# Every phase of a transformer trunk puts the moving operands of its matmuls at another place within 256 bytes

## The reference, cut to what matters

```
for i in range(DEPTH):                                   # 4
    x = x + 0.5 * _swiglu(_rms_norm(x, norm_ffn1[i]), w_gate, w_up, w_down)
    y = mixer(_rms_norm(x, norm_mix[i]))                 # fox, conv, diff, fox
    x = x + y
    x = x + 0.5 * _swiglu(_rms_norm(x, norm_ffn2[i]), w_gate, w_up, w_down)

def _swiglu(h, w_gate, w_up, w_down):                    # D = 1024, D_FF = 2816
    return (jax.nn.silu(h @ w_gate) * (h @ w_up)) @ w_down
```

## Time and profile before

| | us |
|---|---|
| median of 2 runs (1982.21 and 1983.81) | 1983.01 |
| the profiled execution | 1984.66 |
| its span, first to last instruction | 1982.9 |
| TensorE busy in the span | 1955.8 |
| VectorE busy | 1423.5 |
| ScalarE busy | 1044.5 |
| mean granted TensorE clock, share of full speed | 0.996 |

### The profile page before, as it was taken

One profiled execution on the slowest core, in us unless ns is written; L12 is line 12 of the kernel. 1 busy time (PEld: TensorE's weight loads), 2 busy tenths in 40 slices (PEclk: granted clock), 3 DMA queues, 4 the chain that ended last, 5 costly groups with the idle time before them and its releaser, 6 DMA issues.

```text
span 1982.9 us, 29095 instructions
## 1 busy us (share of the span) xinstructions
PE 1955.8 (99%) x12575; PEld 1714.5 (86%) x12575; DVE 1423.5 (72%) x1647; ACT 1044.5 (53%) x1251; POOL 100.8 (5%) x114
## 2 busy tenths in 40 slices
PE   8999999999999998999999999999999999999999
PEld 7888889888888895988888888788888888889887
DVE  8875778875877555876587658887758765778763
ACT  6544656554554444654465455575436544566542
POOL 3000001000200001100100000010000000001000
PEclk9999999999999998999999999999999999999999
DMA  7656435655665683565666553356565655435653
GB/s 243 193 181 193 138 130 166 191 186 189 196 192 181 195 245 74 191 191 187 195 191 191 182 180 128 108 180 191 182 195 187 192 184 179 147 128 172 191 189 108
DMA packets 336669, 350.14 MB, mean 177 GB/s; under 512 B 10125, under 2 KB 331934, under 8 KB 336542
## 3 DMA queue, kind: packets, MB, share of 16 engines
q1 hardware_dynamic: 332046, 343.58, 54.2%
q10 hardware_dynamic: 4496, 4.70, 1.2%
HBM read 346.04 MB, written 2.22 MB: 176 GB/s over the span
## 4 chain that ended last, share of the span: by engine, by line
PE 92%; DVE 3%; ACT 2%; DMA 1%; issue 1%; POOL 1%; ACTq 0%; SPq 0%; DVEq 0%; POOLq 0%
PE banks L1477 49%; PE banks L1482 24%; PE banks L1468 5%; PE banks L1470 4%; PE banks L1469 4%; PE banks L1699 1%; PE banks L1752 1%; DMA u_away<-sb_u_pad 1%; PE banks L1940 1%; DVE sb_w_low L825 1%; PE banks L1719 1%; PE banks L1736 1%; ACT sb_w_high L479 0%; DMA sb_raw<-in_ffn_w_gate 0%; ACT sb_scores L617 0%
## 5 line engine op out<-in xcount | busy, mean ns | idle before, releaser
L825 DVE TENSOR_TENSOR sb_w_low<-sb_raw,sb_w_high 128x2048 fp32r<-128x2048 f32 (+1 forms) x331 | 750.7, 2271 | 209.0 <-ACT sb_w_high L479 208.4
L1477 PE MATMUL banks<-sb_x_both,sb_w_high 128*128 128x512 f32 x2816 | 721.3, 393 | 0.9 <-issue 0.9
L479 ACT ACTIVATE sb_w_high<-sb_raw 128x2048 fp32r<-128x2048 f32 (+1 forms) x331 | 616.5, 1867 | 128.2 <-DMA sb_raw<-in_ffn_w_down 111.2
L1477 PEld LDWEIGHTS banks<-sb_x_both,sb_w_high 128*128 128x128 f32 x2816 | 499.0, 188 | 81.7 <-issue 1.2
L1482 PEld LDWEIGHTS banks<-sb_x_both,sb_w_low 128*128 128x128 f32 x2792 | 385.9, 188 | 35.4
L1482 PE MATMUL banks<-sb_x_both,sb_w_low 128*128 128x256 f32 x2792 | 394.0, 278 | 0.0
L1477 PE MATMUL banks<-sb_h_both,sb_w_high 128*128 128x512 f32 x1408 | 360.1, 394 | 0.0
L1477 PEld LDWEIGHTS banks<-sb_h_both,sb_w_high 128*128 128x128 f32 x1408 | 250.2, 188 | 45.7
L1482 PEld LDWEIGHTS banks<-sb_h_both,sb_w_low 128*128 128x128 f32 x1408 | 190.7, 188 | 17.1
L1482 PE MATMUL banks<-sb_h_both,sb_w_low 128*128 128x256 f32 x1408 | 194.2, 278 | 0.0
L1468 PE MATMUL banks<-sb_x_both,sb_w_high 128*128 128x256 f32 x512 | 146.9, 287 | 0.0
(11 more groups left out here) (235 smaller groups left out, 1943.5 us busy)
## 6 DMA issues: line engine op xcount, KB each, us to landing
sb_raw<-in_ffn_w_up SPq DMA_DIRECT2D x88, 1024.0 KB, 5.4
sb_raw<-in_ffn_w_gate SPq DMA_DIRECT2D x87, 1024.0 KB, 5.4
sb_raw<-in_ffn_w_down SPq DMA_DIRECT2D x64, 1024.0 KB, 5.0
sb_raw<-in_ffn_w_down SPq DMA_DIRECT2D x32, 768.0 KB, 4.3
sb_raw<-in_fox_w_in SPq DMA_DIRECT2D x24, 1024.0 KB, 5.3
sb_raw<-in_conv_w_pw SPq DMA_DIRECT2D x12, 1024.0 KB, 5.5
sb_raw<-in_diff_w_in SPq DMA_DIRECT2D x12, 1024.0 KB, 5.1
sb_raw<-in_fox_w_out SPq DMA_DIRECT2D x8, 1024.0 KB, 4.9
```

Source lines behind the costliest of these rows:

```text
L479: act.activation(slot(w_high, b)[:, 0:width(b)], slot(raw, b)[:, 0:width(b)], ACT.Copy).then_inc(S["high_ready"], 1)
L825: dve.tensor_tensor(slot(w_low, b)[:, 0:width(b)], slot(raw, b)[:, 0:width(b)], slot(w_high, b)[:, 0:width(b)].bitcast(F32), ALU.subtract) ...
L1477: return pe.matmul(pair(bank[at][:, :]), high[:, n * P:(n + 1) * P], m_both, start=first, stop=last, skip_group_check=True)
```

## The change

`x_both` becomes one of 12 views, one for each phase, into `x_room`, a tensor that is 256 elements longer than `x_both` with its shift, and `h_both` one of 12 views into `h_room`. A place is a number of 4-byte elements from the room's beginning. Nothing else is changed: the same instructions in the same order, the same waits, the same transfers.

```
-        sb("shift_x", [P, 16])
-        x_both = sb("x_both", [P, 2, KT, SEQ], F32R)
-        x_high, x_low = x_both[:, 0, :, :], x_both[:, 1, :, :]
+        x_room = sb("x_room", [P, 4368], F32R)
...
-        sb("shift_h", [P, 200])
         with ExitStack() as during_ffn:
-            h_both = during_ffn.enter_context(nc.sbuf_tensor("sb_h_both", [P, 2, FF_TILES, SEQ], F32R))
+            h_room = during_ffn.enter_context(nc.sbuf_tensor("sb_h_room", [P, 11592], F32R))
...
-        sb("shift_o", [P, 24])
...
+        def both_parts_at(room, tiles, place):
+            first, adjacent, apart = place
+            size = tiles * SEQ
+            if adjacent:
+                return room[:, first:first + 2 * size].rearrange("p (t a n) -> p a t n", a=2, n=SEQ)
+            parts = room[:, first:first + 2 * (size + apart)].rearrange("p (a r) -> p a r", a=2)
+            return parts[:, :, 0:size].rearrange("p a (t n) -> p a t n", n=SEQ)
+
+        X_HOME, H_HOME = (16, False, 0), (200, False, 0)
+        X_PLACE = {0: (4, False, 0), 2: (8, False, 0), 3: (12, False, 0), 5: (20, False, 0), 6: (24, False, 0),
+                   8: (28, False, 0), 9: (40, False, 0), 11: (56, False, 0),
+                   4: (48, False, 0), 7: (8, False, 0), 10: (48, False, 0)}
+        H_PLACE = {0: (40, False, 0), 2: (32, False, 0), 3: (36, False, 0), 5: (44, False, 0), 6: (48, False, 0),
+                   8: (28, False, 0), 9: (0, False, 0), 11: (16, False, 0)}
+        x_both = [both_parts_at(x_room, KT, X_PLACE.get(i, X_HOME)) for i in range(len(phases))]
+        h_both = [both_parts_at(h_room, FF_TILES, H_PLACE.get(i, H_HOME)) for i in range(len(phases))]
...
-                    act.activation(x_high[:, t, :], src, ACT.Copy, scale=vec[:, col + t:col + t + 1]
+                    act.activation(x_both[i][:, 0, t, :], src, ACT.Copy, scale=vec[:, col + t:col + t + 1]
...
-                    return both_parts(pair_banks(p) + 2 * which + n, n, high, low, lambda k: x_both[:, :, k, :],
+                    return both_parts(pair_banks(p) + 2 * which + n, n, high, low, lambda k: x_both[i][:, :, k, :],
...
-                        ins = both_parts(2 * (T % 2) + n, n, high, low, lambda k: h_both[:, :, first + k, :],
+                        ins = both_parts(2 * (T % 2) + n, n, high, low, lambda k: h_both[i][:, :, first + k, :],
```

More of the change, by code:

```diff
@@ L570, in high @@
                     act.wait_ge(S["hidden_ready"], PAIRS * f + p + 1)
-                    act.activation(h_both[:, 0, 2 * p:2 * p + 2, :], pair(hidden[:, :]), ACT.Copy
+                    act.activation(h_both[i][:, 0, 2 * p:2 * p + 2, :], pair(hidden[:, :]), ACT.Copy
                                    ).then_inc(S["h_high_ready"], 1)
@@ L869, in x_lows @@
                     src = xT[:, t, :] if i else bank[T][:, t % 2 * SEQ:t % 2 * SEQ + SEQ]
-                    dve.scalar_tensor_tensor(x_low[:, t, :], src, vec[:, col + t:col + t + 1],
-                                             x_high[:, t, :].bitcast(F32), ALU.mult, ALU.subtract
+                    dve.scalar_tensor_tensor(x_both[i][:, 1, t, :], src, vec[:, col + t:col + t + 1],
+                                             x_both[i][:, 0, t, :].bitcast(F32), ALU.mult, ALU.subtract
                                              ).then_inc(S["xlow_ready"], 1)
@@ L1035, in low @@
                     dve.wait_ge(S["h_high_ready"], PAIRS * f + p + 1)
-                    dve.tensor_tensor(h_both[:, 1, 2 * p:2 * p + 2, :], pair(hidden[:, :]),
-                                      h_both[:, 0, 2 * p:2 * p + 2, :].bitcast(F32),
+                    dve.tensor_tensor(h_both[i][:, 1, 2 * p:2 * p + 2, :], pair(hidden[:, :]),
+                                      h_both[i][:, 0, 2 * p:2 * p + 2, :].bitcast(F32),
                                       ALU.subtract).then_inc(S["h_low_ready"], 1)
@@ L1494, in both_parts, with x_parts @@
                 return ins
+            def x_parts(b):
+                x = x_both[max(n for n in range(len(phases)) if starts[n] <= b)]
+                return x[:, 0, :, :], x[:, 1, :, :]
             def columns_half(dst, b, n, tiles=range(KT)):
+                x_high, x_low = x_parts(b)
                 high, low = (slot(t, b).rearrange("p (k n) -> p k n", k=KT) for t in (w_high, w_low))
@@ L1608, in very_first_pair @@
                                 for n in range(2):
-                                    on_both(at + n, n, high[:, k, :], x_both[:, :, k, :], k == 0, False)
+                                    on_both(at + n, n, high[:, k, :], x_both[0][:, :, k, :], k == 0, False)
                             if which == 0 and ks[0] == 0:
@@ L1613, in very_first_pair @@
                                     for k in ks:
-                                        on_high(at + n, n, low[:, k, :], x_high[:, k, :])
+                                        on_high(at + n, n, low[:, k, :], x_both[0][:, 0, k, :])
                         wait_block(which)
@@ L1618, in very_first_pair @@
                                 ins = pe.matmul(bank[at + n][:, SEQ:2 * SEQ], low[:, k, n * P:(n + 1) * P],
-                                                x_high[:, k, :], start=False, stop=k == KT - 1, skip_group_check=True)
+                                                x_both[0][:, 0, k, :], start=False, stop=k == KT - 1, skip_group_check=True)
                         ins.then_inc(S["block_done"], 1)
```

## The result

The changed kernel takes 2004.7 us, the median of two runs (2002.96 and 2006.45), against 1983.01. The ratio is 1.0107, with a 95% interval of 1.0091 to 1.0123. So it is slower by 1.1%, within 2%. My 1993 had the sign right and less than half of the size: +10 us were forecast and +21.7 measured.

A forecast was written before the change was run, and what follows sets the result against it. The prediction took the pace of TensorE's matmuls as the bound. It summed x +10.4, h -0.7 and mixers 0 to +9.7 us, giving 1993 us against the median, with a range of 1968 to 2050.

The forecast's parts named there:

- what bounds it: Whole kernel: time is the number of matmuls times their pace; TensorE is busy for 1955.8 of 1982.9 us.
- the band: Feed-forward matmul pairs: bounds of 338.8 to 353 ns from quick and slow paces; all bounds together give 1948 to 2020 us.
- the step that sized x: Eight feed-forward x parts: new places take h's 348.3 ns a pair, 1.3 us more for a phase, +10.4 us.
- seven h parts costed at 0: Feed-forward h parts outside phase 0: unseen places, left at 0; phase 0's h takes x's pace, -0.7 us.
- the mixers at 0: The mixers' 2880 short matmuls: a mixture of two paces, bounds -6 and +6 us, taken as 0.
- The sum: All parts: 10.4 - 0.7 = +9.7 us, 1994 against the profiled execution, 1993 us against the median.
- Off the 64-byte grid: Rival for feed-forward x and h: starts off multiples of 64 bytes cost 6 ns a run, 2058 us; chance 0.18.
- The loss goes away: Rival for feed-forward pairs: some distances avoid meeting reads, 324 ns a pair, -46 us, 1937 us; chance 0.05.
- The place does nothing: Rival for the feed-forward streams: pace is not set by place, phases repeat, 1983 us within 3; chance 0.14.
- My test of the trace: Feed-forward x windows differ by 0.5 to 3 us, h within 2 of 61.3; durations 388 to 398 and 276 to 283 ns.

The follow-up runs named there:

- The surveys: Two runs of the changed kernel with other place tables, x and h at different distances in each phase; x pairs 344.7 to 354.1 ns at multiples of 16 bytes.
- experiment 2: The kernel before with 32 bytes ahead of everything, so all distances stay but no fp32r operand begins on a multiple of 64 bytes: 1982.69 us, 1.0003.
- experiment 1: The changed kernel with both place tables empty, x at 64 and h at 192 bytes; rooms and o's other place stay: 1984.57 us, 1.0003.
- experiments 10 and 11: The kernel before, then the changed kernel at slow places, with 64 or 32 of 128 staying columns in some phases: no pair under 342.4 ns.
- experiments 3 and 7: The kernel before with only the weights 32 bytes further: 2004.65 us; the changed kernel with all feed-forward x and h at 68 bytes: 2043.09 us.
- experiment 4: The kernel before with only w_high, the staying operand of the long matmuls, 32 bytes further: 2004.37 us in one run.

## Why the prediction was right or wrong

**Right: what bounds it.** The time is the number of matmuls times their pace, and the place changes only the pace. TensorE's busy time and the span grew by the same 18 us, and no new wait came.

**Right, nearly: the band.** Pairs of 338.8 to 353 ns were the bounds, and all phases of the changed kernel lie from 346.3 to 353.3. The upper bound was 2 ns low by its own rows: it took 118 ns for a slow short matmul where rows 6 go to 120. (The loss of a long matmul by rows 4 and 5 is 16 to 21 ns, not 16 to 20; nothing hangs on it.) Off the 16-byte lines the band does not hold (359.8), but the change goes to no such place.

**Wrong: the step that sized x.** I took h's 348.3 ns for x's unseen places, "because it is the only other place at which these rows show the same lines". x's eight places have 348.1 to 353.0 ns and 350.5 on the mean, 5.8 ns above 344.7 where I had 3.7 (strictly 3.6). The windows grew by 16.0 us in place of 10.4. The surveys show why the one other row misled. The two rows stood for the two best distances of 16 (x has 344.7 and 346.7 at them), and the mean of the 16 is 350.1. The row with the same lines was a sample of one, and not a neutral one; the middle of my own band was no better (346). What could have been drawn from before is less than I drew: that the effect exists, and its bounds.

**Wrong: seven h parts costed at 0.** The eight cost 2.8 us, where -0.7 was forecast. Phase 0 went to 64 and gained 0.3, the other seven lost 3.1. For these I had argued from "h's own value is near the band's upper middle", where in fact it was one of h's three best distances of the twelve run.

**Nearly right: the mixers at 0.** -1.6 us for their x parts and +1.4 for o, as read from one execution of each kernel. The x stretches hold waits, so this is no price of places: in experiment 2, with all distances as before, the conv phase's x part was 3.5 us shorter than before. o at 64 in place of 192 costs about 0.3 us in each mixer, in experiment 1 too.

**The sum.** 16.0 + 2.8 - 0.2 = 18.6 us, less the 0.3 at the start, explain the two profiled spans. The medians are 21.7 apart, and the profiled executions 18.3: the profiled one of before (1984.66) is above its median and that of the changed kernel (2002.96) below its own. The 3 us between are within what the runs of one kernel differ by (before: 1980.21 to 1989.08 over 19 runs). So about half of what the forecast lacked is the size for x, a little under a third the h parts, and the rest is this difference of executions.

**The rivals.** *Off the 64-byte grid*: wrong, experiment 2. It had a true relative at 16 bytes, which I had set aside because all new places are multiples of 16. *The loss goes away*: wrong at all distances tried, and by experiments 10 and 11 most of the loss does not shrink with the columns of the other read. *The place does nothing*: wrong, experiments 3 and 7. The Trainium skill's rule that led there (TensorE: Matmul & The Clock Gate, step 1 of "Step-by-step: what each phase is for", two independent read ports) does not hold to the last percent here: moving only the weights made x's windows 1.7 us longer.

**My test of the trace.** I asked for x windows that differ and h windows within 2 us of 61.3, and both came. I also asked for durations of at most 398 and 283 ns; the long ones reach 400 (x and h in phase 9) and the short ones 288 (phase 11).

## What to carry to other kernels

Where TensorE streams fp32r operands back to back, start the moving operand on a 16-byte line, and then try its distance from the staying operand modulo 256 bytes: in this kernel the first was worth 3% (68 against 64) and the second 1%, with no instruction changed. Give each repeated phase of one kernel a different place and read each window: the price of a place seen in one phase held when all eight had it (2041 forecast, 2043 measured). If the trace holds one or two places only, they bound nothing about the others; take their difference as a sign that there is an effect, not as its size.

## What the runs showed of the hardware that was not expected

- A moving operand that begins 4 bytes into a 16-byte line: 356.8 to 362.4 ns a pair against 344.7 to 354.1 at line starts, whatever its distance from the weights. 8 bytes: 353.6 to 360.0. 12 bytes: 347.4 to 349.5.
- Among line starts, the distance modulo 256: from 344.7 (64) to 354.1 (208), repeated at 256 and 320; 64 and 192 are unchanged when everything moves by 32 bytes.
- Streams of short matmuls of the same shape and at the same place can run at 113.3 or 117.7 ns. In experiment 4, moving only the staying operand of the long matmuls made nearly all of x's short ones slow.
- The base of the loss is still open. At the best place fp32r runs at no less than 113 ns for 256 columns, with 32 staying columns too, where plain float32 takes 216, almost exactly two cycles a column; the starts of the gate matmuls are 216 ns apart too. No run here separates the type from the rate at which it asks for data.
